# Last three operations of the group norm carried into the next pair of heads, with their operands in used rows of k and v

## The reference, cut to what matters

```python
y = jnp.moveaxis(ys, 0, 1)
mu = jnp.mean(y, axis=-1, keepdims=True)
var = jnp.mean(jnp.square(y - mu), axis=-1, keepdims=True)
yn = ((y - mu) * lax.rsqrt(var + GN_EPS)).reshape(B, T, W) * lnx_w + lnx_b
bonus = jnp.sum(r_h * k_h * r_k, axis=-1, keepdims=True) * v_h
out = (yn + bonus.reshape(B, T, W)) * g
```

## Time and profile before

| | us |
|---|---|
| median of 3 executions (lowest, highest) | 2415.4 (2415.17, 2415.6) |
| the profiled execution, whole | 2415.23 |
| its span | 2413.5 |
| PE busy | 2351.0 (97%) |
| DVE busy | 1473.5 (61%) |
| ACT busy | 879.6 (36%) |
| PE's share of the chain that ended last | 82% |
| a 1 MB unit of w_in, from issue to landing, median | 5.3 |

### The profile page before, as it was taken

One profiled execution on the slowest core, in us unless ns is written; L12 is line 12 of the kernel. 1 busy time (PEld: TensorE's weight loads), 2 busy tenths in 40 slices (PEclk: granted clock), 3 DMA queues, 4 the chain that ended last, 5 costly groups with the idle time before them and its releaser, 6 DMA issues.

```text
span 2413.5 us, 48839 instructions
## 1 busy us (share of the span) xinstructions
PE 2351.0 (97%) x19616; PEld 2252.7 (93%) x19616; DVE 1473.5 (61%) x2125; ACT 879.6 (36%) x1048; POOL 131.3 (5%) x203
## 2 busy tenths in 40 slices
PE   8999999999999999999999998999999999999999
PEld 6899989898888888888999988999999999999998
DVE  5644544566677666776535457665666666566676
ACT  6443344343332233322434344333333333333334
POOL 3000011000000010000001010000000000000003
PEclk9999999999999999999999999999999999999999
DMA  7554487342333243332445633444444444444443
GB/s 267 185 165 142 160 285 251 97 140 90 99 100 96 85 137 96 100 96 86 151 153 160 197 105 105 157 140 143 158 151 149 147 156 140 143 157 151 152 145 110
DMA packets 282189, 346.67 MB, mean 144 GB/s; under 512 B 6957, under 2 KB 240733, under 8 KB 280907
## 3 DMA queue, kind: packets, MB, share of 16 engines
q1 hardware_dynamic: 271883, 307.66, 39.6%
q0 software_dynamic: 9712, 36.30, 4.5%
q10 hardware_dynamic: 464, 0.79, 0.1%
HBM read 333.83 MB, written 10.89 MB: 143 GB/s over the span
## 4 chain that ended last, share of the span: by engine, by line
PE 82%; DVE 10%; issue 4%; ACT 1%; DMA 1%; DVEq 1%; SPq 0%; ACTq 0%
PE bank L246 19%; PE bank L255 19%; PE bank L247 19%; PE bank L227 4%; PE bank L229 4%; PE bank L228 4%; PE bank L1193 3%; DVE work L911 2%; ACT hi L211 1%; DVE lo L218 1%; PE bank L1210 1%; PE bank L511 1%; DVE work L1025 1%; PE bank L512 1%; PE bank L518 1%
## 5 line engine op out<-in xcount | busy, mean ns | idle before, releaser
L218 DVE TENSOR_TENSOR lo<-raw,hi 128x2048 fp32r<-128x2048 f32 x286 | 655.8, 2293 | 502.9 <-ACT hi L211 485.6
L246 PE MATMUL bank<-ah,hi 128*128 128x320 f32 x3200 | 957.4, 313 | 0.2 <-DVE al L532 0.2
L247 PE MATMUL bank<-al,hi 128*128 128x320 f32 x3200 | 945.9, 309 | 0.0
L211 ACT ACTIVATE hi<-raw 128x2048 fp32r<-128x2048 f32 x286 | 548.0, 1916 | 935.1 <-PE bank L255 681.1
L246 PEld LDWEIGHTS bank<-ah,hi 128*128 128x128 f32 x3200 | 601.0, 188 | 15.4 <-issue 13.3
L247 PEld LDWEIGHTS bank<-al,hi 128*128 128x128 f32 x3200 | 601.4, 188 | 0.4
L255 PE MATMUL bank<-ah,lo 128*128 128x320 f32 x3200 | 545.4, 311 | 2.5 <-DVE lo L218 2.5
L255 PEld LDWEIGHTS bank<-ah,lo 128*128 128x128 f32 x3200 | 486.4, 188 | 7.4 <-DVE lo L218 4.1
L227 PE MATMUL bank<-bh,hi 128*128 128x320 f32 x704 | 218.7, 311 | 0.2 <-DVE work L2410 0.2
L229 PE MATMUL bank<-bh,lo 128*128 128x320 f32 x704 | 217.5, 309 | 0.0
L228 PE MATMUL bank<-bl,hi 128*128 128x320 f32 x704 | 217.5, 309 | 0.0
(11 more groups left out here) (386 smaller groups left out, 2090.7 us busy)
## 6 DMA issues: line engine op xcount, KB each, us to landing
raw<-in_w_in SPq DMA_DIRECT2D x98, 1024.0 KB, 5.3
raw<-in_w_up SPq DMA_DIRECT2D x88, 1024.0 KB, 5.1
raw<-in_w_down SPq DMA_DIRECT2D x44, 1024.0 KB, 5.1
raw<-in_w_branch SPq DMA_DIRECT2D x24, 1024.0 KB, 5.5
raw<-in_w_out SPq DMA_DIRECT2D x16, 1024.0 KB, 5.4
raw<-in_w_mem_k SPq DMA_DIRECT2D x8, 1024.0 KB, 5.8
raw<-in_w_mem_v SPq DMA_DIRECT2D x8, 1024.0 KB, 5.2
work<-in_cache_mem_k POOLq DMA_DIRECT2D x8, 1024.0 KB, 6.0
```

What stands on the lines that cost most here:

```text
L211: act.activation(hi[c % NS][:, :], raw[c % 2][:, :], ACT.Copy).then_inc(S("hi_done"), 1)
L218: dve.tensor_tensor(lo[c % NS][:, :], raw[c % 2][:, :], hi[c % NS][:, :], ALU.subtract)\
L246: pe.matmul(out, w, xh[:, 8 * h + k, :], start=h + k == 0, stop=False)
L247: pe.matmul(out, w, xl[:, 8 * h + k, :], start=False, stop=False)
```

## The change

- The root, the reciprocal and the two operations behind it no longer use `zc` and `bon`. The squares, var + eps and the root lie in `row_(i + 8)` (k of the pair, used by then); the bonus goes by ACT to `t_ck`, is multiplied by v into `row_(i + 16)` (v of the pair, copied by then), and is gated there; `ym` gets slot 15 of its own. The squares' moving operand of PE's var product is `row_(i + 8)`.
- ACT's copy of the bonus waits for `gated_out` no more.
- The reciprocal, the product and the sum become `norm_out`, which DVE runs in the next pair, between the key scores and RT1; the result of pair n goes to `row_(n + 1)`, and the branch stage reads rows 1 to 8. The first pair runs it too, on memory whose result is not used; behind the last pair it stands at the start of `branch_dve`.
- On DVE, `weights_low(0)` moves from before RT1 to behind B4, the bonus product from behind B4 to before BCt; `prepare_norm` and the last line of `prepare_k` (now `prepare_av`) move to between Z2 and Z3; `prepare_rest` moves behind the copy of y; `weights_low(5)` stands ahead of `branch(1, 1)`.
- ACT's root waits for tr0 instead of mean, and so stands behind the conversion of unit 5.

```diff
@@ -716,13 +716,13 @@
...
         zc3 = zc.rearrange("p (c k) -> p c k", c=NC)
-        v_, alp, be, ka, rh, t_x, t_ad, t_bd, t_bo, t_rt, t_bk, ka_t, t_ck, bon = [wslot(n) for n in range(2, 16)]
+        v_, alp, be, ka, rh, t_x, t_ad, t_bd, t_bo, t_rt, t_bk, ka_t, t_ck = [wslot(n) for n in range(2, 15)]
...
         vtm = wk[:, 8 * T + 512:8 * T + 1024].rearrange("p (b v) -> p b v", b=NB)
-        y_, ym, ysq = t_x, zc[:, 0:T], zc[:, T:2 * T]
+        y_, ym = t_x, wslot(15)
@@ -835,10 +835,22 @@
...
             vv.do(dve.tensor_scalar(av, av, 0.5, 0.5, ALU.mult, ALU.add))
-            tmp = t_bd if first else row_(j + 15)
+            tmp = t_bd if first else row_(j + 7)
             vv.do(dve.tensor_scalar(tmp, av, -1.0, pcol("k_a", j), ALU.add, ALU.mult))
             vv.do(dve.scalar_tensor_tensor(out=row_(j + 8), in0=tmp, scalar=1.0, in1=row_(j + 8), op0=ALU.add, op1=ALU.mult))
+            if first:
+                prepare_av(dve, vv)
+        def prepare_av(dve, vv):
             vv.do(dve.tensor_tensor(av, kkv, av, ALU.mult))
+        def norm_out(dve, vv, j):
+            dve.wait_ge(S("gn_root"), j + 1)
+            vv.do(dve.reciprocal(row_(j + 8), row_(j + 7)))
+            vv.do(dve.tensor_tensor(ym, ym, row_(j + 8), ALU.mult))
+            vv.do(dve.tensor_tensor(row_(j), ym, row_(j + 15), ALU.add), "gated_out")
@@ -867,6 +879,7 @@
...
             vv.do(dve.memset(st_[0], 0.0), "ring_out")
+            vv.do(dve.memset(ym, 0.0), "gn_root")
             vv.do(dve.memset(st_[1], 0.0), "gated_out")
@@ -941,16 +954,16 @@
...
                 plain(t_b2, "B2")
+                dve.wait_ge(S("turned_out"), OUT0_A + N_OUT_A * i + OUT_A["bonus"] + 1)
+                tt(row_(i + 16), t_ck, row_(i + 16), ALU.mult)
                 for name, cs in (("BCt", TURNED), ("BCs", UPRIGHT)):
...
                     part(t_ck, name, 64 * len(cs), cs, m_in, "ring_out")
-                weights_low(0)
+                norm_out(dve, vv, i)
                 plus(t_rt, "RT1")
                 plain(t_bd, "B4")
-                dve.wait_ge(S("turned_out"), OUT0_A + N_OUT_A * i + OUT_A["bonus"] + 1)
-                tt(bon, bon, row_(i + 16), ALU.mult)
-                prepare_norm(dve, vv, i + 1)
+                weights_low(0)
                 plus(t_rt, "RT2")
@@ -966,6 +979,8 @@
...
                 plus(zc, "Z2", 512)
+                prepare_norm(dve, vv, i + 1)
+                prepare_av(dve, vv)
                 plus(zc, "Z3", 512)
@@ -1000,16 +1015,16 @@
...
                 prepare_kk(dve, vv, i + 2)
-                prepare_rest(dve, vv, i + 1)
                 dve.wait_ge(S("y_ps"), i + 1)
                 vv.do(dve.tensor_copy(y_, bank[6][:, 0:T]), "y_out")
+                prepare_rest(dve, vv, i + 1)
                 ps("g")
-                vv.do(dve.scalar_tensor_tensor(out=bon, in0=bon, scalar=pcol("lnx_b", i), in1=bank[6][:, 0:T],
+                vv.do(dve.scalar_tensor_tensor(out=row_(i + 16), in0=row_(i + 16), scalar=pcol("lnx_b", i), in1=bank[6][:, 0:T],
                                                op0=ALU.add, op1=ALU.mult))
...
                                                op0=ALU.mult, op1=ALU.add), "ring_out")
-                tt(ysq, ym, ym, ALU.mult, "ym_sq")
+                tt(row_(i + 8), ym, ym, ALU.mult, "ym_sq")
                 ps("trp")
@@ -1018,14 +1033,10 @@
...
                 ps("var")
-                vv.do(dve.tensor_scalar(ysq, pbank("var")[:, 0:T], 1.0 / HD, GN_EPS, ALU.mult, ALU.add), "ring_out")
+                vv.do(dve.tensor_scalar(row_(i + 8), pbank("var")[:, 0:T], 1.0 / HD, GN_EPS, ALU.mult, ALU.add), "ring_out")
                 prepare_ops(dve, vv, i + 1)
+                weights_low(5)
                 branch(1, 1)
-                dve.wait_ge(S("gn_sqrt"), i + 1)
-                vv.do(dve.reciprocal(ysq, ysq))
-                tt(ym, ym, ysq, ALU.mult)
-                tt(row_(i), ym, bon, ALU.add, "gated_out")
-                weights_low(5)
@@ -1046,8 +1057,7 @@
...
                 ps("bonus")
-                act.wait_ge(S("gated_out"), j)
-                aa.do(act.activation(bon, pbank("bonus")[:, 0:T], ACT.Copy), "turned_out")
+                aa.do(act.activation(t_ck, pbank("bonus")[:, 0:T], ACT.Copy), "turned_out")
                 act.wait_ge(S("wkv_ps"), PS0 + NPR * i + PR["ssq"] + 1)
@@ -1083,9 +1093,10 @@
...
             if ps:
-                ps("mean")
+                ps("tr0")
                 act.wait_ge(S("ring_out"), OUT0 + N_OUT * j)
-                aa.do(act.activation(ysq, ysq, ACT.Sqrt), "gn_sqrt")
+                act.activation(row_(j + 7), row_(j + 7), ACT.Sqrt).then_inc(S("gn_root"), 1)
+                act.wait_ge(S("gn_root"), j + 1)
                 for m in range(2):
@@ -1095,7 +1106,7 @@
...
         def wkv_act(act, aa, n):
-            with aa.loop(4 * n, 4 * n + 4, {"act": 2, "low_out": 2, "exps": 3, "kk_root": 1, "v_copied": 1, "gn_sqrt": 1, "turned_out": N_OUT_A}) as i:
+            with aa.loop(4 * n, 4 * n + 4, {"act": 2, "low_out": 2, "exps": 3, "kk_root": 1, "v_copied": 1, "turned_out": N_OUT_A}) as i:
                 units = [0]
@@ -1349,7 +1360,7 @@
...
                 wait("sam_ready", i + 1)
-                wait("gated_out", i + 1)
+                wait("gated_out", i + 2)
                 sam_, vtm_ = [x.rearrange("p b v -> p (b v)") for x in (sam, vtm)]
@@ -1391,7 +1402,7 @@
...
                 wait("ym_sq", i + 1)
-                end(pe.matmul(o[:, 0:T], blk[:, :], ysq, start=True, stop=True))
+                end(pe.matmul(o[:, 0:T], blk[:, :], row_(i + 8), start=True, stop=True))
                 state_turned(0)
@@ -1892,8 +1903,8 @@
...
             tile_ready(act, U_BR[2] - 1)
-            act.wait_ge(S("gated_out"), KW + 1)
-            aa.do(act.activation(bh[:, :, :], rw[:, 0:KW, 0:T], ACT.Copy), "bh_ready")
+            act.wait_ge(S("gated_out"), KW + 2)
+            aa.do(act.activation(bh[:, :, :], rw[:, 1:KW + 1, 0:T], ACT.Copy), "bh_ready")
             with act.Fori(8, 11) as i:
@@ -1914,8 +1925,9 @@
...
         def branch_dve(dve, vv):
+            norm_out(dve, vv, KW)
             dve.wait_ge(S("bh_ready"), 2)
-            vv.do(dve.tensor_tensor(bl[:, :, :], rw[:, 0:KW, 0:T], bh[:, :, :], ALU.subtract), "bl_ready")
+            vv.do(dve.tensor_tensor(bl[:, :, :], rw[:, 1:KW + 1, 0:T], bh[:, :, :], ALU.subtract), "bl_ready")
             with vv.loop(8, 11, {"gate_free": 4}) as i:
```

## The result

Five executions each: 2424.0 us median (2422.0 to 2429.84) against 2415.6 us (2415.17 to 2417.17); ratio 1.0039, interval 1.0024 to 1.0053. The change made the kernel slower by 8 us where 7 us less were forecast, and its times spread more. The profiled execution took 2422.0 us, the fastest of the five, so what follows is the least that was lost. A standstill here is a stretch in which PE computes nothing.

What follows compares the result with a forecast made beforehand. PE, 82% of the chain, was taken as the bound, with only its idle time to win or lose. 18.9 + 2.4 + 0.4 - 14.8 = 6.9 us off 2415.23 gave 2408.3 us, range 2403.5 to 2413.0.

Steps and rivals of the forecast that it cites:

- what bounds the kernel: Eight pairs: PE busy 578.2 of 602 us; only its 23.8 us idle can be won or lost.
- RT1's price: PE's wait before vkt/vks for RT1's addition grows 1.85 us in all eight pairs: 14.8 us lost.
- Front of the pairs: Bonus product to key scores: waits for root of ssq and A2's copy vanish, 7 x 2.7 = 18.9 us gained.
- rival 1: ACT, pair's end: table load costs 1.28 us more in its new place, 4.4 us lost, 2412.7 us; chance 0.09.
- rival 2: ACT: unit 5's conversion, its weights landing late, delays root and copies, 11.6 us lost, 2419.9 us; chance 0.07.
- rival 3: Front waits go, but PE stands elsewhere (late filler weights or DVE late at ABt): 2415 us; chance 0.08.
- Copy of y: prepare_rest no longer precedes the copy of y, which PE waits for: 2.4 us gained, bounds 0 and 2.4.
- Behind Z2, loads: DVE's added 3.3 us behind Z2 fit its 4.04 us idle, and shifted weight loads land in time: no cost.
- New waits: norm_out's wait for the previous pair's root, the later branch and PE's next gated_out wait all have ample lead.
- Behind the last pair: PE waits about 2 us for unit 2's hi instead of 2.48 us for lo: 0.4 us gained.

Runs made afterwards that it cites:

- e1: Changed kernel with three 128x320 products added on PE in its wait before vkt/vks, results overwritten: 2410.4 us, ratio 0.9972.
- e3: Changed kernel with norm_out and weights_low(0) exchanged, so the norm's three operations run behind B4's copy: 2398.9 us, ratio 0.9927.
- e6: e3 with prepare_rest put back in front of the copy of y: 2404.3 us, ratio 0.9954.
- e5: e3 with the last pair's handover split: seven rows rounded and unit 2 converted during the norm, eighth row after it: 2394.6 us, ratio 0.9913.
- e4: Kernel before the change with three 128x320 operations added on DVE ahead of RT1's addition, results unused: 2442.9 us, ratio 1.0110.
- e2: Changed kernel with one of the three filler steps ahead of RT2 moved ahead of vkt/vks: 2404.2 us, ratio 0.9951.

## Why the prediction was wrong, step by step

- **The step that failed** is the second sentence of what bounds the kernel, that "nothing but PE's idle time can be won or lost", and with it RT1's price as a term that grows with the length of the wait alone. The sum had no term for the clock, although one standstill of 2.48 us in its own rows had lowered it. The wait itself came as forecast (0.20 to about 2.05 us in the text, 2.28 us measured in the first pair, with bounds of 1.2 to 2.3 us). The price did not: from the first pair's bonus product to the eighth pair's var product the changed kernel takes 5.4 us more than before, while its undisturbed lengths (1.25 us less in seven pairs, by the waits about 1.55 us more in the first) make 7.2 us less. The falls within the pairs thus cost 12.6 us; the 15.4 us of the clock's column are an upper end. Why they are more is not shown: in nearly all of the low stretches PE is recorded as busy. e1's trace gives 12.6 us for the same stretch, its median 13.6 us for the whole. None of the rivals contained it; the kernel became slower, to which the text gave 0.06, for a reason that this chance did not stand for.
- **Front of the pairs**: right. 9.81 to 7.04 us, 2.77 a pair (forecast 2.7).
- **ACT and the table load** (rival 1): refuted. The load starts at 772.45 and the root at 773.75, 1.30 us. The Trainium skill (ScalarE: Activation LUTs, What ACT_TABLE_LOAD costs) adds some 1.38 us of drain to a switch; no room for it is in these rows, nor in the earlier trace rows. PE does not wait at the bonus product.
- **Unit 5's conversion holding ACT** (rival 2, the slower one): refuted though the kernel did become slower. The conversion runs at 767.83, released by PE, not by its load.
- **The gain doesn't arrive** (rival 3): refuted as it was put. The front's gain arrived, and A2's wait did not come back.
- **RT1's price in waiting**: right in total, 16.9 - 2.3 = 14.6 us against 14.8, but by luck in part. Five pairs grew by 2.07 to 2.09 us, not 1.85, and the seventh by 1.8; the third and fifth by only 1.1 and 1.4, as PE had stood 0.80 and 0.50 us within the key scores ("issue", of which the profile shows no cause) and so came later to the wait. The third pair's 1.26 us and the 2.38 and 2.37 us of the sixth and eighth lie outside the 1.8 to 2.3 us that were to hold in all eight. What the sum had too small are gaps: 0.37 us ahead of the reciprocal and 0.26 us ahead of the sum, where it had 0.23 and, inside its 3.51 us, 0.14.
- **Copy of y**: right in kind, mis-sized: 4.2 us by the traces of e3 and e6, above its bound of 2.4.
- **Behind Z2, loads**: right, no wait appeared.
- **New waits**: the two idle times of 1.3 us together within the key scores are new and stand in no term; the third pair, which has the longer one, takes 73.85 us like the fourth, so it cost nothing there.
- **Behind the last pair**: the forecast gain of 0.4 us is there as a distance (var product to unit 2's first product, 19.6 us before, 19.3 after), but for another reason: PE waits 3.6 us, not 2. The 19.6 us before held a fall of the clock, which I had read as ordinary speed, so that PE came earlier to the new wait than I worked out; and the wait of 3.6 us lowered the clock once more, behind it (1.7 us by the column). e5 shows that the long wait and the fall can both go.

That a standstill of some 2 us lowers the clock is shown by e1 (same instructions elsewhere, PE busy: no fall) and e4 (standstill added alone: falls). Why it did not in the fourth pair of the changed kernel, nor in the second and fourth of e4, stays open; these views show no difference there. Nor is it known why one fall lasted twice as long as another.

## What to carry to other kernels

Where standstills lower an engine's clock, count them by their length as well as by their sum: here two of 1.3 us a pair cost 2.8 us, and one of 2.3 us in their place cost 2.1 us and, in six of eight pairs, 1.6 to 3.0 us more. Before moving work into a gap, read the granted clock in short stretches behind the longest existing waits of the trace; the kernel before had one of 2.48 us, with its price in the rows. Over a long stretch the fall disappears: the changed kernel's clock still reads 0.96 over the first pair and 0.99 over the whole. When the bottleneck must wait, give it filler from later (e2), or find the place where the moved work is hidden (e3).

## What the runs showed of the hardware

- TensorE's granted clock fell to the lower level (1.2 GHz) at the end of unbroken idle times of 1.86 to 2.38 us, or up to 2 us behind it, in 12 of 15 such places within the pairs (7 in the changed kernel, 8 in e4), and was back 3 to 7 us after it fell; behind idle times of up to 1.31 us, in the eight pairs of all kernels, it stayed at 2.4 GHz unless one of the longer ones followed. One fall cost 1.6 us where the column lost 1.7, and 2.6 to 3.0 us where it lost 3.4 (pairs of the changed kernel against those of e1). The Trainium skill (TensorE: Matmul & The Clock Gate, Part 1) says that the gate follows how busy PE has been; e1 agrees: with PE kept busy the clock read 1.00 throughout the pairs.
- Where executions of one kernel differ, the mean clock goes with the time: the changed kernel took 2422.0 to 2424.0 us at 0.990 and 2426.8 to 2429.8 us at 0.987, e5 2394.2 to 2394.7 us, all at 0.996. That standstills make the times spread is not shown: e4, with eight of 1.87 us, spread by 2.2 us, and e1, with none above 0.8 us in the pairs, by 5.7 us.
- A recorded idle time of PE of 0.27 us cost 0.43 us at its place (e6 against e3).
